# Two tables streamed beside gathers: other tile quotas per step, a gate stage of 22 steps, and second-table loads of four tiles

## The chip, the core and the metric

One core of one Trainium2 chip runs the whole kernel. The metric is the device time of one execution in microseconds (us); the profiled execution is one such execution, with every engine's instructions and every DMA packet recorded. TensorE is PE (its weight loads PEld), VectorE DVE, ScalarE ACT, GpSimd POOL, and SyncE SP, which here does nothing but wait for semaphores and issue DMAs in program order.

## What is computed

One layer of an encoder block: a token mixer (a causal convolution branch and a stick-breaking attention branch, gated and projected) with a layer norm, and then PEER, a retrieval of single-neuron experts, which is what this change is about:

```python
s1, s2 = q1 @ keys_1.T, q2 @ keys_2.T            # 8 heads, 128 keys each
v1, i1 = top_k(s1, 16); v2, i2 = top_k(s2, 16)
top_s, pos = top_k(v1[:, None] + v2[None, :], 16)
idx = (i1 * 128 + i2)[pos]                       # one of 16384 experts
gate = softmax(top_s)
u, vv = expert_u[idx], expert_v[idx]             # rows of 1024 float32
act = gelu(einsum('td,thkd->thk', x, u))
y = einsum('thk,thkd->td', gate * act, vv)
x = layer_norm(ALPHA * x + y)
```

There are 1024 tokens in 8 blocks of 128.

## The kernel before

Six of the eight token blocks get their experts by **gather**. The work of a block and a head is a turn of 8 steps (`TURNS` = 48 turns, `STEPS` = 8, so 384 steps). In each step POOL gathers two experts for each of 128 tokens, rows of 8 KB that hold u and v together (`indirect_dma_start`, L975), into a ring of 8 places, four steps deep; DVE forms the dot products (`dots`, L2430), ACT the weights (`expert_weights`, L1806 to L1815), and PE adds the weighted v rows to the block's sum (`experts`, L1258). A ring place is free when PE has used it.

The last two blocks (`DENSE` = 2) are computed **densely** beside turns 32 to 47, without gathers: all 16384 rows of both tables are streamed through. Steps are counted from there as s, from 0 to 127, and each engine does in each step what `dense` gives it, in program order beside its part of the gathered work.

- **First table** (`u_tile`, L1496): 128 tiles of 128 experts; the products with the 256 tokens go through a gelu (L1957) into `act_out` and, but for the last two chunks, out to DRAM (`store_act`). SP loads two tiles per transfer (`load_u`, L848) into six places. `u_first(s)` says which tiles belong to step s: 128 tiles over `U_STEPS` = 94 steps, evenly. A pair is loaded when tile 2m - 6 + 1 has been used (`u_used`). The third pair waits for `y_read`, since its place holds data of the gathered block 3 until then.
- **Score slabs**: beside turns 30 to 38 PE also forms queries and scores for further heads (L1219, L1243). The two halves of a slab are loaded by SP (`load_slab_late`, L730). The first half may be loaded when the first half of the slab before has been read (`q_psum`), the second when its scores are done (`score_psum`). Slab 13 (`LATE_SLAB + 2`) is the one that PE wants first at step 0. Here SP issues its loads at n = `USLOTS - 1`, behind the third pair.
- **Picks and gates**: from step 0 DVE picks the top experts of the dense blocks (`dense_pick`, four steps per head and block, 64 steps). At `G_STEP0` = 64 PE turns the picks (`turn_picks`). Then the gates are spread to the full table, in 64 groups of four tokens over `G_STEPS` = 24 steps: DVE writes two one-hot matrices (`hot_group`, L2525 and L2529) into one of two places `hot`, PE multiplies them (`g_group`, L1509), ACT copies the result into `g_out` (L1967), and SP stores each block of eight groups, 2 MB, to DRAM (`store_g`, L857). `g_out` has two places; ACT fills one again when its store has landed. SP issues a store at tile `u_first(g_full(i)) + USLOTS` of its own loop, behind the `load_u` of that point.
- **Between the tables**: SP issues the rest of the stores, waits until they have landed, loads the gates of the first two chunks of eight tiles (`load_g`, L879, pieces of 1 KB per partition), and then the first second-table tiles.
- **Second table** (`v_tile`, L332 to L334 by `split_products`): 128 tiles over `V_STEPS` = 31 steps, evenly (`v_first`). Each v tile is rounded by ACT (`round_v`, L1978), the rest is formed by DVE (L2554), and PE makes 12 matmuls of 512 columns. Four tiles at a time the activations are multiplied by their gates (DVE, L2566, two steps ahead of use), rounded by ACT (L1989) and split by DVE (L2548). SP loads two tiles per transfer (`load_v`, L868) into four places of two; a place is loaded again when its two tiles have been used, so pair m waits for 2m - 6 used tiles. Every four tiles come 0.5 MB of activations (`load_act`, L888) and 0.5 MB of gates (`load_g`). In SP's order at one count of used tiles these two come first, and then the pair.
- **Tail**: three steps (`TAIL`) without table tiles, in which DVE finishes the dense blocks and the last gathered one.

ACT and DVE prepare v tiles two ahead of the step (`AHEAD`), and ACT's rounding has four places (`VHI`), so tile n is rounded only after tile n - 4 is used.

## Time and profile before

| | us |
|---|---|
| median of 3 runs | 3004.21 (2998.26 to 3004.87) |
| profiled execution | 3014.1 |
| its span, first to last instruction | 3012.3 |
| PE / DVE / ACT / POOL busy | 2616.7 / 2327.7 / 1223.7 / 971.8 |
| moved by DMA | 1100.76 MB, mean 365 GB/s |

A busy PE is not PE at its peak: ends of matmuls are modelled. "DMA share" is the mean busy share of the 16 DMA engines (it can come out a little over 1), the clock is the one granted to PE, 1.00 being 2.4 GHz and 0.50 being 1.2 GHz. What stands in brackets behind an instruction is the idle time of its engine before it and what ended it.

### The profile page before, as it was taken

Reading aid. Unit: us, or ns where it says so; the run is one execution under the profiler, and the core shown is the slowest. Engines: PE = TensorE matmul, PEld = TensorE weight load, DVE = VectorE, ACT = ScalarE, POOL = GpSimd, SP = SyncE. Lnnn points to the kernel's source line nnn. Section 1 sums busy time; section 2 is a strip of 40 time slices with the busy share of each in tenths; the row PEclk is TensorE's granted clock in tenths of the full one; section 3 lists DMA queues with packets and bytes.
Section 4 is the critical chain, followed back from the end, with each engine's and each line's share of the span. In section 5 each row is a group of like instructions: output and inputs, shape, how many; then the busy total and the mean of one; then the engine's idle time right before and its main releaser. Section 6 shows DMA issues by size and latency. Waiting matters only on the chain. (4 is left out here: it accounts for less than half of the span.)

```text
span 3012.3 us, 53462 instructions
## 1 busy us (share of the span) xinstructions
PE 2616.7 (87%) x20618; PEld 1518.2 (50%) x20618; DVE 2327.7 (77%) x4875; ACT 1223.7 (41%) x3048; POOL 971.8 (32%) x888
## 2 busy tenths in 40 slices
PE   9899978787887767768888869999998997999997
PEld 7677433232332333323333326666676775766774
DVE  7965577999879899976767867767788884877776
ACT  3254143233345555533333423333244332544454
POOL 0000144444445555544343522223232222211221
PEclk9999999889997777779998989999999999999998
DMA  4113699999999999999999989999999999999995
GB/s 165 63 56 140 240 403 419 413 404 417 412 419 405 420 411 420 419 420 421 421 418 406 419 336 383 397 394 401 400 416 375 397 412 411 386 392 369 410 393 210
DMA packets 175382, 1100.76 MB, mean 365 GB/s; under 512 B 17829, under 2 KB 34341, under 8 KB 52778
## 3 DMA queue, kind: packets, MB, share of 16 engines
q0 software_dynamic: 110592, 805.36, 65.3%
q1 hardware_dynamic: 64554, 292.16, 24.5%
q8 instruction: 160, 2.62, 0.3%
q14 instruction: 76, 0.62, 0.1%
HBM read 1061.79 MB, written 35.65 MB: 364 GB/s over the span
## 5 line engine op out<-in xcount | busy, mean ns | idle before, releaser
L975 POOL DMA_INDIRECT arena_high<-uv_dram,idx_now x768 | 929.3, 1210 | 1665.9 <-PE ps L1258 1525.2
L2430 DVE SCALAR_TENSOR_TENSOR arena_high<-arena_low,arena_high 128x1024 f32<-128x1024 f32 x768 | 922.4, 1223 | 267.4 <-DMA arena_high<-uv_dram,idx_now 261.5
L1258 PE MATMUL ps<-arena_high 32*32 32x512 f32 x12288 | 493.5, 671 | 282.5 <-ACT arena_high L1815 278.1
L1496 PE MATMUL ps<-arena_low 128*128 128x256 f32 x2048 | 463.7, 382 | 0.0
L1496 PEld LDWEIGHTS ps<-arena_low 128*128 128x128 f32 x2048 | 384.0, 190 | 109.4 <-issue 46.0
L1806 ACT ACTIVATE gcol<-hcol 128x2 f32<-128x2 f32 x384 | 77.6, 202 | 824.4 <-DVE arena_high L2430 820.0
L1258 PEld LDWEIGHTS ps<-arena_high 32*32 32x32 f32 x12288 | 94.8, 107 | 481.6 <-ACT arena_high L1815 384.6
L1219 PE MATMUL ps<-arena_low 128*128 128x512 f32 (+1 forms) x512 | 242.0, 616 | 14.3 <-DMA arena_low<-slabs_dram 14.3
L332 PE MATMUL ps<-wv_hi_bytes,w_hi_bytes 128*128 128x512 f32 x512 | 207.6, 406 | 19.4 <-DVE v_lo_bytes L2554 13.1
L1815 ACT ACTIVATE arena_high<-arena_high,wcol 128x32 f32<-128x32 f32 x768 | 204.9, 314 | 12.5
L334 PE MATMUL ps<-wv_hi_bytes,w_lo_bytes 128*128 128x512 f32 x512 | 202.3, 395 | 0.0
L1808 ACT ACTIVATE wcol<-gcol,arena_high 128x1 f32<-128x1 f32 x768 | 184.2, 287 | 12.6
L1219 PEld LDWEIGHTS ps<-arena_low 128*128 128x128 f32 x512 | 98.1, 203 | 168.6 <-issue 139.8
L1957 ACT ACTIVATE arena_low<-ps 128x512 f32<-128x512 f32 x64 | 38.2, 596 | 320.9 <-PE ps L1496 320.9
L333 PE MATMUL ps<-x_lo_bytes,w_hi_bytes 128*128 128x512 f32 x384 | 152.0, 396 | 0.0
L332 PEld LDWEIGHTS ps<-wv_hi_bytes,w_hi_bytes 128*128 128x128 f32 x512 | 98.2, 192 | 70.4 <-issue 30.7
L1393 PE MATMUL ps<-arena_low 128*128 128x512 f32 x256 | 126.4, 640 | 0.0
L332 PE MATMUL ps<-x_hi_bytes,w_hi_bytes 128*128 128x512 f32 x256 | 103.9, 406 | 7.2 <-DVE x_lo_bytes L2116 7.1
L334 PEld LDWEIGHTS ps<-wv_hi_bytes,w_lo_bytes 128*128 128x128 f32 x512 | 97.9, 191 | 21.2
L970 POOL CAST idx_now<-arena_high 128x8 uint32<-128x8 f32 x96 | 39.1, 407 | 209.4 <-DVE arena_high L2416 209.0
L2554 DVE TENSOR_TENSOR x_hi_bytes<-arena_low,wv_hi_bytes 128x1024 fp32r<-128x1024 f32 x64 | 76.4, 1223 | 39.0 <-ACT wv_hi_bytes L1978 38.5
L334 PE MATMUL ps<-x_hi_bytes,w_bytes 128*128 128x512 f32 x256 | 101.0, 395 | 0.0
(264 smaller groups left out, 4002.4 us busy)
## 6 DMA issues: line engine op xcount, KB each, us to landing
arena_low<-ut_dram SPq DMA_DIRECT2D x64, 1024.0 KB
arena_high<-vt_dram SPq DMA_DIRECT2D x32, 1024.0 KB, 12.7
arena_low<-vt_dram SPq DMA_DIRECT2D x32, 1024.0 KB
arena_low<-spread_dram SPq DMA_DIRECT2D x32, 512.0 KB
acts_dram<-arena_low SPq DMA_DIRECT2D x14, 1024.0 KB
arena_low<-acts_dram SPq DMA_DIRECT2D x28, 512.0 KB
arena_low<-slabs_dram SPq DMA_DIRECT2D x11, 1152.0 KB
arena_high<-uv_dram,idx_now POOLq DMA_INDIRECT x768
```

The source lines that it names most:

```text
L332: nc.tensor.matmul(out, w_hi, x_hi, start=first, stop=False)
L333: nc.tensor.matmul(out, w_hi, x_lo, start=False, stop=False)
L334: return nc.tensor.matmul(out, w_lo, x_hi, start=False, stop=last)
L975: pool.indirect_dma_start(out=ring[:, s % RING, :], out_offset=None, in_=uv_d, in_offset=bass.IndirectOffsetOnAxis(ap=idx_now[:, s:s + 1], ...
L1219: last = nc.tensor.matmul(ps[:, q_half_bank(i, half), j0 * P:j1 * P], w[:, k, half, :], x1T[:, j0:j1, k, :], start=(k == 0), stop=(k == KD ...
L1258: last = nc.tensor.matmul(ps[out:out + QUAD, y_bank(t // PH) + turn, :], diag[rows, s % DIAGS, :], ring[rows, s % RING, cs], start=fresh, ...
L1393: last = nc.tensor.matmul(ps[:, 4 + g, :], w_mix_late[m % 2][:, o:o + P], xT_late[:, k, :], start=(k == 0), stop=(k == KD - 1))
L1496: last = nc.tensor.matmul(ps[:, 5 + n % 4 // 2, o:o + 2 * P], u_slot[n % USLOTS][:, k, :], x1T[:, BLK - DENSE:BLK, k, :], start=(k == 0), ...
L1806: steps.link(nc.scalar.activation(gcol[:, s0:s0 + 2], hcol[:, s0:s0 + 2], ACT.Gelu))
L1808: last = nc.scalar.activation(wcol[:, s:s + 1], gcol[:, s:s + 1], ACT.Copy, scale=gates[:, t % (BLK * PH), s:s + 1])
L1815: nc.scalar.activation(diag[:, s % DIAGS, :], quad_eye, ACT.Copy, scale=wcol[:, s:s + 1]).then_inc(diag_ready, 1)
L2430: last = nc.vector.scalar_tensor_tensor(out=ring[:, s % RING, 0:D], in0=x1[c][:, j, :], scalar=1.0, in1=ring[:, s % RING, 0:D], op0=ALU.mu ...
```

## The change

Five edits. (1) The two halves of slab 13 are issued at n = `USLOTS - 2`, before the third u pair. (2) `u_first` and `v_first` follow weights: steps 0 to 55 take 133 parts each, the gate steps 113, the other first-table steps 205; second-table steps 0 to 24 take 467 and the last eight 130. First-table steps are 92, second-table steps 33. (3) Gate groups take 22 steps instead of 24, PE's and ACT's from step 65 and DVE's from step 64, with four `hot` places. (4) The first four gate loads are issued at tile `u_first(G_BACK) + USLOTS - 2` in SP's loop over the first table, `G_BACK` being 88. (5) The second table is loaded four tiles per transfer, with 16 KB in a row in DRAM, into two places of 16 KB per partition. Load m waits for 4m - 4 used tiles, and in SP's order comes before the activation and gate loads of the same count.

```diff
-V_STEPS = 31
+V_STEPS = 33
+V_FULL = 25
...
-G_STEP0 = PICK0 + DENSE * PH * PICK_PARTS - U0
-G_STEPS = 24
+G_STEP0 = PICK0 + DENSE * PH * PICK_PARTS - U0 + 1
+G_STEPS = 22
+HOTS = 4
 KEPT = 2
+G_BACK = G_STEP0 + G_STEPS + 1
...
+def u_share(s):
+
+    G = U0 + s
+    if G < PICK0 + 7 * STEPS:
+        return 133
+    return 113 if G_STEP0 <= s < G_STEP0 + G_STEPS else 205
...
 def u_first(s):
-    return NT * s // U_STEPS
+    return NT * sum(u_share(i) for i in range(s)) // sum(u_share(i) for i in range(U_STEPS))
+
+
+def v_share(v):
+    return 467 if v < V_FULL else 130
...
 def v_first(v):
-    return NT * v // V_STEPS
+    return NT * sum(v_share(i) for i in range(v)) // sum(v_share(i) for i in range(V_STEPS))
...
-        v_pair = [at(kib, 2, D) for kib in (168, 176, 64, 72)]
+        v_quad = [at(kib, 4, D) for kib in (168, 64)]
...
-        hot = at(16, 2, 4, 2 * P)
+        hot = [at(kib, 4, 2 * P) for kib in (16, 20, 28, 32)]
...
-                if m == VSLOTS // 2 - 1:
+                if m == 1:
                     wait_again(sp_eng, u_used, NT)
-                if m >= VSLOTS // 2:
-                    wait_again(sp_eng, v_used, 2 * m - VSLOTS + 2)
-                sp_eng.dma_start(v_pair[m % (VSLOTS // 2)], vt_d[v_expert(2 * m) // 2, :, :, :]).then_inc(v_in[m % (VSLOTS // 2)].sem, 16)
+                if m >= 2:
+                    wait_again(sp_eng, v_used, 4 * m - VSLOTS + 4)
+                sp_eng.dma_start(v_quad[m % 2], vt_d[v_expert(4 * m) // 4, :, :, :]).then_inc(v_in[m % 2].sem, 16)
...
             for n in range(NT):
+                if n == USLOTS - 2:
+                    for half in range(2):
+                        load_slab_late(LATE_SLAB + 2, half)
                 if n % 2 == 0:
                     load_u(n // 2)
...
+                if n == u_first(G_BACK) + USLOTS - 2:
+                    for c in range(2):
+                        for part in range(2):
+                            load_g(c, part)
...
-            for c in range(2):
-                for part in range(2):
-                    load_g(c, part)
...
-                if n % 2 == 0:
-                    load_v(n // 2)
+                if n % 4 == 0:
+                    load_v(n // 4)
...
-                if s == G_STEP0:
+                if s == G_STEP0 - 1:
                     for j in range(DENSE):
                         turn_picks(j)
...
-                wait_again(act, v_in[n // 2 % (VSLOTS // 2)], 16 * (n // VSLOTS + 1))
+                wait_again(act, v_in[n // 4 % 2], 16 * (n // VSLOTS + 1))
...
-                if i >= 2:
-                    wait_again(dve, g_psum, i - 1)
+                if i >= HOTS:
+                    wait_again(dve, g_psum, i - HOTS + 1)
...
-                o = s - G_STEP0
+                o = s - G_STEP0 + 1
```

## Rows read from the trace of the kernel before

**Rows 1.** Windows by stage: length, busy us (instructions) per engine, granted clock, DMA share, GB/s.

```profile
1773.00:1787.00 14.00, 0.00 (x0) 0.00 (x0) 13.21 (x45) 1.22 (x5) 0.00 (x0) 0.60 0.98 406
1787.00:1794.00 7.00, 6.93 (x11) 3.16 (x12) 6.65 (x20) 0.00 (x0) 0.00 (x0) 0.58 0.06 23
1794.00:2228.00 434.00, 434.00 (x3331) 291.94 (x3329) 307.77 (x895) 156.57 (x427) 119.15 (x123) 1.00 0.97 390
2228.00:2295.00 67.00, 61.08 (x543) 42.04 (x528) 51.71 (x144) 23.76 (x67) 21.22 (x21) 0.95 1.01 422
2295.00:2508.00 213.00, 198.40 (x1728) 158.31 (x1727) 183.60 (x503) 86.99 (x239) 50.87 (x51) 1.00 0.97 391
2508.00:2566.00 58.00, 39.91 (x352) 28.52 (x338) 22.91 (x52) 15.99 (x42) 13.48 (x15) 0.87 1.01 412
2566.00:2937.00 371.00, 353.69 (x2222) 264.06 (x2223) 288.55 (x377) 185.36 (x295) 78.23 (x63) 0.97 0.99 390
2937.00:2983.00 46.00, 44.88 (x291) 33.85 (x305) 30.46 (x35) 21.27 (x37) 7.67 (x6) 1.00 0.78 308
2983.00:3012.00 29.00, 10.21 (x152) 1.79 (x120) 20.30 (x30) 9.96 (x19) 0.00 (x0) 0.64 0.14 55
```

**Rows 2.** Groups of instructions, 2295 to 2508: count | busy, mean ns | idle before, releaser.

```profile
L2529 DVE TENSOR_SCALAR arena_low<-iota,arena_low 128x128 f32<-128x128 f32 x248 | 69.6, 347 | 0.0
...
L2525 DVE TENSOR_TENSOR arena_low<-iota,arena_low 128x512 f32<-128x512 f32 x62 | 42.7, 688 | 27.6 <-PE ps L1509 27.2
...
L1509 PE MATMUL ps<-arena_low 128*128 128x128 f32 x496 | 65.8, 281 | 14.6 <-DVE arena_low L2529 14.5
```

**Rows 3.** The page of the whole execution: its first line.

```profile
span 3012.3 us, 53462 instructions
```

**Rows 4.** Timeline of PE, 1744 to 1800 and the last u tiles: start, us, line, count.

```profile
1748.06 2.84 PE L1219 MATMUL ps<-arena_low 128*128 128x512 f32 x6
...
1762.56 2.05 PE L1243 MATMUL ps<-arena_low 128*128 128x128 f32 x16
...
1787.07 6.57 PE L1219 MATMUL ps<-arena_low 128*128 128x512 f32 x8 [14.34 <-DMA arena_low<-slabs_dram]
...
1798.09 3.70 PE L1219 MATMUL ps<-arena_low 128*128 128x512 f32 x8
...
2538.54 7.17 PE L1496 MATMUL ps<-arena_low 128*128 128x256 f32 x32
```

**Rows 5.** Chain of waits in the second table: two expert groups, a step apart.

```profile
2603.94 1.07 PE ps L1258 x32
...
2616.12 1.07 PE ps L1258 x32
```

**Rows 6.** Timeline of SP around step 0: start, us until the last issue, line, DMA, count.

```profile
1715.85 58.53 SPq L848 DMA_DIRECT2D arena_low<-ut_dram  x3
1774.42 0.91 SPq L730 DMA_DIRECT2D arena_low<-slabs_dram  x2
```

**Rows 7.** Chain of waits between the tables, in order of time: start, us, what.

```profile
2512.63 18.24 DMA spread_dram<-arena_low
...
2532.46 10.56 SPq L879
2543.07 20.28 DMA arena_high<-vt_dram
```

**Rows 8.** The copies into `g_out` (L1967), all of them: what ACT waited for.

```profile
  PE ps L1509: 71.0, 63
```

**Rows 9.** Timeline of DVE in the same stretch.

```profile
2558.00 1.23 DVE L2566 TENSOR_TENSOR arena_low<-arena_low 128x1024 f32<-128x1024 f32 x1 [21.86 <-DMA arena_low<-spread_dram]
```

**Rows 10.** Rounding and subtraction of v tiles: count: duration ns min/median/max, first, last start.

```profile
L1978 ACT ACTIVATE wv_hi_bytes<-arena_low x64: 1038/1045/1065, 2573.4 to 2972.0; 128x1024 fp32r<-128x1024 f32 x64
...
L2554 DVE TENSOR_TENSOR x_hi_bytes<-arena_low,wv_hi_bytes x64: 1217/1224/1228, 2574.8 to 2973.1; 128x1024 fp32r<-128x1024 f32 x64
```

**Rows 11.** DMAs from `vt_dram`, two tiles each: time from issue to landing, us.

```profile
DMA to landing us min/median/max: 8.0/12.7/16.7
```

More of the change, by code:

```diff
@@ L603, in build @@
         g_stored = [Again(wv_in, 16), Again(bv_in, 16)]
-        v_in = [Again(wbranch_in[i], 32) for i in range(VSLOTS // 2)]
+        v_in = [Again(wbranch_in[i], 32) for i in range(2)]
         v_rounded = Again(gates_done, 16)
@@ L891, in _ @@
             for n in range(NT):
+                if n == USLOTS - 2:
+                    for half in range(2):
+                        load_slab_late(LATE_SLAB + 2, half)
                 if n % 2 == 0:
                     load_u(n // 2)
-                for i in range(LATE_SLAB + 2, len(SLABS)):
-                    s0 = (i - LATE_SLAB - 3) * STEPS
-                    if n == (USLOTS - 1 if s0 < 0 else u_first(s0 + 2) + USLOTS):
+                for i in range(LATE_SLAB + 3, len(SLABS)):
+                    s0 = (i - LATE_SLAB - 3 + 32) * STEPS - U0
+                    if n == u_first(s0 + 2) + USLOTS:
                         load_slab_late(i, 0)
-                    if n == (USLOTS - 1 if s0 < 0 else u_first(s0 + 7) + USLOTS):
+                    if n == u_first(s0 + 7) + USLOTS:
                         load_slab_late(i, 1)
@@ L1508, in g_group @@
                 for q in range(4):
-                    last = nc.tensor.matmul(ps[:, (4, 7)[i % 2], q * P:(q + 1) * P], hot[:, i % 2, q, 0:P],
-                                            hot[:, i % 2, q, P:2 * P], start=True, stop=True, skip_group_check=True)
+                    last = nc.tensor.matmul(ps[:, (4, 7)[i % 2], q * P:(q + 1) * P], hot[i % HOTS][:, q, 0:P],
+                                            hot[i % HOTS][:, q, P:2 * P], start=True, stop=True, skip_group_check=True)
                 last.then_inc(g_psum.sem, 1)
@@ L1997, in dense @@
                 s = G - U0
-                if s == G_STEP0:
+                if s == G_STEP0 - 1:
                     for j in range(DENSE):
@@ L2520, in hot_group @@
                     wait_again(dve, picks_ready, DENSE)
-                if i >= 2:
-                    wait_again(dve, g_psum, i - 1)
+                if i >= HOTS:
+                    wait_again(dve, g_psum, i - HOTS + 1)
                 j = i // (P // 4)
                 t0 = 4 * i - j * P
-                nc.vector.tensor_tensor(hot[:, i % 2, :, 0:P], iota128[:, :].unsqueeze(1).to_broadcast([P, 4, P]),
+                nc.vector.tensor_tensor(hot[i % HOTS][:, :, 0:P], iota128[:, :].unsqueeze(1).to_broadcast([P, 4, P]),
                                         picksT[:, j, 1, t0:t0 + 4].unsqueeze(2).to_broadcast([P, 4, P]), ALU.is_equal)
@@ L2528, in hot_group @@
                     t = t0 + q
-                    last = nc.vector.tensor_scalar(hot[:, i % 2, q, P:2 * P], iota128[:, :], picksT[:, j, 0, t:t + 1],
+                    last = nc.vector.tensor_scalar(hot[i % HOTS][:, q, P:2 * P], iota128[:, :], picksT[:, j, 0, t:t + 1],
                                                    picksT[:, j, 2, t:t + 1], ALU.is_equal, ALU.mult)
@@ L2787 @@
         "ut": arr(peer_u).reshape(NKEY // 2, 2, NKEY, KD, P).transpose(0, 4, 1, 3, 2).reshape(NKEY // 2, P, 2, D),
-        "vt": arr(peer_v).reshape(NKEY // 2, 2, NKEY, D).transpose(0, 2, 1, 3),
+        "vt": arr(peer_v).reshape(NKEY // 4, 4, NKEY, D).transpose(0, 2, 1, 3),
         "cols": np.concatenate([col(bi[0:col_v]), col(bi[col_g:]), col(arr(conv_b_pw2)), col(arr(conv_b_dw)),
```

## The prediction

> **What bounds the kernel now.** I read the windows by stage first [rows 1]: they show, per stage, how long PE was busy, its granted clock and how full the 16 DMA engines were. From 1794 on both are full at once: PE 434.00 of 434 with DMA share 0.97, then 61 of 67 with 1.01, 198 of 213 with 0.97, 354 of 371 with 0.99. So neither alone "is" the bound; a change can only win back time in which both stood still or one stood for a reason of its own. There are four such places: 1773 to 1794, where PE did nothing for 14.3 us and DMA then stood still (23 GB/s); the gate stage 2295 to 2508 with 14.6 us of PE idle before its gate matmuls [rows 2]; the joint 2508 to 2566 between the two tables (PE 40 of 58 us); and the end of the second table, 2937 to 2983, where DMA falls to 0.78. After 2983 a serial tail of 29 us remains that the change does not touch. The profiled execution took 3014.1 us around a span of 3012.3 [rows 3]; the median of the timed runs is 3004.2. I sum against the span and carry the difference over to the median.
>
> **Prices.** Two first-table tiles (u tiles) in a row take 7.17 us of PE, 3.6 each [rows 4]. One step and four second-table tiles (v tiles) take 12.18 us, from one expert group at 2603.94 to the next at 2616.12, of which the expert group is 1.07: 2.78 us for a v tile [rows 5]. A gate group is 65.8/62 = 1.06 us on PE and (69.6+42.7)/62 = 1.81 us on DVE [rows 2]. A gather step and a u tile move 2.1 and 0.52 MB; at the 390 to 420 GB/s of [rows 1] that is 5.1 and 1.3 us of DMA. All bytes stay as they are.
>
> **1. Slab 13 ahead of the third u pair.** SP sits in L848 from 1715.85 until the pair is issued about 1774.0, since that pair waits for `y_read`; the two halves of slab 13 come behind it at 1774.42 [rows 6], and PE, in order, waits 14.34 us for them and then runs its first eight passes at the low clock, 6.57 us instead of 3.70 [rows 4]. Moved ahead, the halves wait for slab 12's use alone: its first half is read for the last time about 1749 to 1751, its scores end at 1764.6 [rows 4]. Both halves are on their way 10 to 25 us earlier, and PE needs the first at 1773 and the second some three steps later. Queued behind the moved waits is only the third pair, which has to wait until 1774 anyway. Gain 14.3 + 2.9 = 17.2 us on PE; nothing else is late there, since DMA stood still too. Bounds: 10 (the second half late by a few us) to 17.
>
> **2. Tiles by step.** The quota sums give 74 u tiles after step 55 (76 before), 92 after step 64 (88 at this point before), 117 after the last gate step, 128 after step 91 (before 93). Steps 0 to 55 are paced by PE [rows 1]: 1773 to 2228 is 455 us, minus 17.2, minus two tiles 7.1: 431. DMA needs for this stretch some 56 x 5.1 + 70 x 1.3 + slabs and stores near 45 = 422, so it just keeps up. Steps 56 to 64: 67 us before with 12 tiles and two gate groups; now 18 tiles and none: +6 x 3.6 - 2.1 = 86.5, less part of the 6 us that PE idled: 83 (78 to 88).
>
> **3. Gates in 22 steps with four `hot` places.** Before, DVE stands 27.6 us in front of L2525 for PE, and PE 14.6 us for DVE [rows 2]: with two places each waits for the other in turn. With four places, and DVE one step ahead, this falls away. What is late next: DVE needs 183.6 - one step's 3.3 + two groups 3.6 = 184 us, PE 25 tiles x 3.65 + 64 x 1.06 + 22 x 1.1 = 183, DMA 22 gather steps, 25 tiles, 16.8 MB of gate stores: 79 MB at 410 = 193. Floor 188 to 193 against 213 (for 23 steps and 31 tiles). But ACT may fill a `g_out` place again only when its store has landed, and a store takes 18.24 us [rows 7]. SP issues it after a `load_u` that waits for PE: by the new quotas blocks 0, 4 and 5 leave only with the first tile of the step after the one in which they do now, while a block of eight groups takes 2.75 steps instead of 3. Today no fill waits for DMA: the only releaser of L1967 is PE [rows 8]. For these blocks I get 5 to 10 us each of ACT standing, with PE behind it at the next group, partly absorbed because DVE and DMA run on: +10 (0 to 25). Stage: 203.
>
> **4. Gate loads before the last u tiles.** Before, u tiles ended at 2545.7 [rows 4], and the first v tile waited for a chain: store 18.24, SP's wait in L879, v pair 20.28 [rows 7]; DVE stood 21.86 us at L2566 for the gate load, with the next dots behind it in order [rows 9]. Now tiles 117 to 127 and five expert groups are 11 x 3.6 + 5.4 = 45 us. The wait for the stores moves into SP's queue at tile 123. Behind it stand the last two `load_u`, and behind these v quad 0. PE has tiles to about 24 us past tile 117; store (18) and 2 MB of gate pieces in 1 KB runs (10 to 18, they share the engines with gathers) and one u pair (3) make 31 to 39. PE stands 8 to 16 us, instead of the 18 before; but quad 0 lands while the last four u tiles run. Joint: 57 (48 to 68), against 58 with two fewer tiles and one step more before.
>
> **5. Second table.** Steps 0 to 24 take 4.70 tiles, the last eight 1.31. PE work is 128 x 2.78 + 33 x 1.07 = 391 us (before 389, measured 417 from 2566 to 2983). DMA's work moves from the last steps to where PE works: a long step asks for 5.1 + 4.7 x 1.95 = 14.3 us of DMA and 14.1 of PE, a short one 7.6 and 4.7 (a v tile with its act and gate pieces is 0.79 MB, 1.95 us), while the gathers end four steps before the end. What DMA lost in 2937 to 2983, 0.22 x 46 = 10 us, can mostly be used. Against it, a place of four tiles is only asked for again when all four are used, so the next tile but three has 4 x 2.78 + 1.07 = 12.2 us from issue to use, where a pair had six tiles, 17.7 us. To this belong rounding and subtraction, 1.05 + 1.22 [rows 10]. **The landing of 2 MB is in no row.** Lower bound: the quickest pair, 8.0 us for 1 MB; upper: the slowest, 16.7, plus 1 MB more at 410 GB/s, 2.6: 19.3 [rows 11]. I take 10.5, near the low end, for the slow pairs stand behind an act and a gate load issued in the same burst, and the quad comes ahead of them: 2 MB at full rate 5.1 plus at most one step's gathers beside it 5.1, and a little to start. Use is then possible at 12.8: 0.6 us late, and as two places alternate, half of it counts: 29 x 0.3 = 8.7 us. What is behind it: ACT's rounding in order blocks its next expert weights, DVE's L2554 its next dots. Act and gate pieces now land after the quad; the multiply L2566 sometimes has three tiles (9 us) of lead instead of four. -10 + 2 + 8.7 = +0.7: 417 stays (400 to 450). Taking 32 issues away from SP is worth nothing: SP mostly waits.
>
> The Trainium skill ("DMA: Bandwidth & Descriptors", section "Anatomy of one DMA — SWDGE (gpsimd) path") puts one transfer at about 2.0 us plus bytes over 436 GB/s. By that estimate a quad lands in 6.8 us and is never late, and the 8.7 us of my sum would be 0, which is the v stage of rival (c) below. The row speaks against using it here: a lone pair would be 4.4 by the same fit, and the quickest measured is 8.0, the median 12.7 [rows 11].
>
> **Sum.** 1773 + 431 + 83 + 203 + 57 + 417 + 29.5 = 2993.5 against 3012.3: -18.8. Median: 3004.2 - 18.8 = 2985.4, say 2985.5.
>
> **Rivals.** (a) *Quads come late, slower.* If a quad lands in 14.5 us, use is at 16.8, the period of four tiles is (12.2 + 16.8)/2 = 14.5 instead of 12.2: +2.3 x 29 = 67, instead of my 9, of which some 15 are hidden as DMA is the slower anyway: +43 on the sum, 3028. It decides from a landing of about 12.7 us, where (15.0 - 12.2)/2 x 29 = 41 less 15 eats my 19. For it: median pair 12.7, multiply already waits for gate pieces in the saturated stretch; against: place in the burst, and that gathers per tile fall by 12%. 0.12. (b) *Only the start is gained:* stores hold up the gates by 20, the joint gives nothing, v stage +5: -17 + 15 = about 3002. 0.13. (c) *Every cover holds:* gates at 190, joint 50, v stage at DMA's floor 405: 2985.5 - 13 - 7 - 12 = 2954. 0.13. (d) *The slab move does nothing*, because half 1 lands late and PE stands as long: +14, 2999.5. 0.03. My forecast, as summed, 0.59.
>
> **Chances and range.** Likeliest 2985.5; its own bounds (start 10 to 17, gates 0 to 25, joint 48 to 68, v 400 to 450) give about 2966 to 3003. With 2 in 10 left out, below from (c) and above from (a): 2962 to 3010. A measurement can tell about 0.2%, 6 us. Faster than 2998.2: forecast, (c) and a little of (b): 0.76. Within 0.2%: 0.13. Slower than 3010.2: 0.11.
>
> **What would show it.** Right: no PE wait for a slab near 1773, and DMA never at rest there; L2525 no longer released by PE; first v tile near 2547; no step of the last eight over 8 us. Wrong: `arena_low<-spread` stores releasing L1967 for more than 25 us in all; PE idle before L332 over 50 us with `vt_dram` behind ACT's rounding; quads landing above 13 us. If steps 0 to 55 don't get shorter by 17 us besides the two tiles, DMA and not PE paced them.

## The result, and the profile after

The kernel after takes 3035.24 us (median of 5 runs, 3030.86 to 3041.04), the kernel before in the same comparison 3004.87 us (2998.26 to 3011.85): ratio 1.0094, 95% interval [1.0082, 1.0106]. The change makes the kernel slower by 0.9%, some 28 us; the prediction said 2985.5 us. The profiled execution took 3041.0 us.

Lines have moved: L848, L868, L879 and L1219 of before are L863, L883, L894 and L1238 after, L1258, L1496, L1509 are L1277, L1515, L1528, L1967, L1978 and L1989 are L1986, L1997 and L2008, the weights L1806 to L1815 are L1825 to L1834, L2430, L2525, L2554, L2566 are L2449, L2544, L2573, L2585, and PE's L332 to L334 are L347 to L349.

The page of the kernel after, against [rows 3] and [rows 11]: its first line, the group of the u tiles (its idle time at the end), and the DMA issues (size of one, median us from issue to landing).

```profile
span 3038.9 us, 53432 instructions
...
L1515 PE MATMUL ps<-arena_low 128*128 128x256 f32 x2048 | 465.8, 384 | 16.6 <-DMA arena_low<-ut_dram 16.6
...
arena_high<-vt_dram SPq DMA_DIRECT2D x16, 2048.0 KB, 9.8
arena_low<-vt_dram SPq DMA_DIRECT2D x16, 2048.0 KB, 10.5
arena_low<-spread_dram SPq DMA_DIRECT2D x32, 512.0 KB, 13.8
```

The four-tile loads (quads) land in about 10 us, which is what the prediction had assumed. The windows by stage, in the columns of [rows 1]:

```profile
1773.00:1794.00 21.00, 21.00 (x148) 12.71 (x160) 19.24 (x62) 3.40 (x12) 3.75 (x4) 0.98 1.01 408
1794.00:2205.00 411.00, 411.00 (x3181) 275.65 (x3149) 309.11 (x897) 154.11 (x420) 121.14 (x119) 1.00 0.99 400
2205.00:2283.00 78.00, 76.66 (x609) 57.38 (x608) 51.34 (x143) 26.18 (x69) 21.15 (x21) 1.00 1.01 416
2283.00:2476.00 193.00, 178.82 (x1617) 143.74 (x1616) 181.43 (x502) 82.16 (x236) 59.30 (x49) 0.97 0.97 400
2476.00:2541.00 65.00, 46.48 (x342) 35.48 (x337) 17.22 (x34) 12.08 (x33) 10.90 (x12) 0.87 0.88 349
2541.00:2944.00 403.00, 359.37 (x2113) 267.07 (x2114) 282.28 (x373) 181.94 (x278) 65.92 (x54) 0.95 0.88 341
2944.00:3010.00 66.00, 56.65 (x464) 38.29 (x479) 42.51 (x57) 28.23 (x66) 25.71 (x20) 0.97 0.99 388
3010.00:3038.00 28.00, 9.52 (x152) 1.79 (x120) 20.09 (x30) 10.50 (x20) 0.00 (x0) 0.67 0.18 71
```

Up to the first v tile the kernel after is ahead: 2541.0 against 2565.8. The bubble at 1773 is gone (PE 21 of 21 us, DMA 1.01). Then the second table takes 468.6 us (2541.0 to 3009.6) instead of 417.0, and in it neither engine nor DMA is full: PE 359 of 403, DMA share 0.88 and 341 GB/s where [rows 1] had 0.99 and 390. So waits pace it, and not the throughput of PE or DMA.

The waits of that stretch (2541 to 2955; engine, what, releaser: total us, times, longest) point at the loads. ACT, before its rounding, stood 48.6 + 46.1 us for v loads in 24 waits, 10.0 us at the longest. The kernel before has such waits too, 66.0 us in 31 between 2566 and 2983, but none over 7.5 us. The rows after:

```profile
ACT w_hi_bytes L2008 <- DVE arena_low L2585: 75.8, 24, 8.5
DVE x_hi_bytes L2573 <- ACT wv_hi_bytes L1997: 54.7, 17, 8.7
ACT wv_hi_bytes L1997 <- DMA arena_high<-vt_dram: 48.6, 12, 9.2
DVE x_lo_bytes L2573 <- ACT wv_hi_bytes L1997: 48.1, 13, 8.8
ACT wv_hi_bytes L1997 <- DMA arena_low<-vt_dram: 46.1, 12, 10.0
```

One such wait, step by step. Quad 12 (tiles 48 to 51) is issued at 2696.50, when tile 43 has been used, and lands at 2706.8. The timeline of ACT (start, us, what, count, and in brackets the idle time before it):

```profile
2706.81 1.06 ACT L1997 ACTIVATE wv_hi_bytes<-arena_high 128x1024 fp32r<-128x1024 f32 x1 [9.19 <-DMA arena_high<-vt_dram]
2710.30 1.06 ACT L2008 ACTIVATE w_hi_bytes<-arena_low 128x1024 fp32r<-128x1024 f32 x1 [2.43 <-DVE arena_low L2585]
2712.59 0.20 ACT L1825 ACTIVATE gcol<-hcol 128x2 f32<-128x2 f32 x1 [1.23 <-DVE arena_high L2449]
2712.83 0.48 ACT L1827 ACTIVATE wcol<-gcol,arena_high 128x1 f32<-128x1 f32 x2
2713.34 0.53 ACT L1834 ACTIVATE arena_high<-arena_high,wcol 128x32 f32<-128x32 f32 x2
2713.78 2.94 ACT L1997 ACTIVATE wv_hi_bytes<-arena_high 128x1024 fp32r<-128x1024 f32 x3
```

of DVE:

```profile
2707.91 1.23 DVE L2573 TENSOR_TENSOR x_lo_bytes<-arena_high,wv_hi_bytes 128x1024 fp32r<-128x1024 f32 x1 [8.83 <-ACT wv_hi_bytes L1997]
2709.05 1.22 DVE L2585 TENSOR_TENSOR arena_low<-arena_low 128x1024 f32<-128x1024 f32 x1
2710.18 1.22 DVE L2449 SCALAR_TENSOR_TENSOR arena_high<-arena_low,arena_high 128x1024 f32<-128x1024 f32 x1
```

and of PE:

```profile
2709.28 0.47 PE L347 MATMUL ps<-wv_hi_bytes,w_hi_bytes 128*128 128x512 f32 x1 [0.64 <-DVE x_lo_bytes L2573]
...
2716.13 0.79 PE L347 MATMUL ps<-wv_hi_bytes,w_hi_bytes 128*128 128x512 f32 x1 [3.85 <-DVE x_lo_bytes L2573]
2716.72 0.63 PE L348 MATMUL ps<-x_lo_bytes,w_hi_bytes 128*128 128x512 f32 x1
```

Tile 48, the quad's first, is the last that ACT and DVE prepare in their step. PE gets it only 0.64 us late. But ACT and DVE stood some 9 us for it, and behind it, in program order, come the multiply (2709.05), the rounding of its result (2710.30), the next step's two dots (from 2710.18) and weights (2712.59), and only then the rounding of tiles 49 to 51 (2713.78), 7.0 us after they landed. So the tile that is late is 49, by 3.85 us. Over the whole stage PE's idle time before the first matmul of tiles 4m, 4m + 1, 4m + 2 and 4m + 3 adds up to 10.1, 18.9, 14.4 and 4.6 us: most of it before tiles that are not the first of their quad. The Trainium skill ("PSUM — Partial Sum Buffer", section "Engine vs sequencer instructions") calls the queues of ScalarE and VectorE strictly first in, first out. These rows agree: tile 49 was there at 2706.8 and was rounded at 2713.78, behind all that stood before it.

### The profile page after: what moved, and what is told of

Same layout as the page of the kernel before. It is cut to its first block and busy times, and to the rows that moved or that the text cites. A ratio compares the mean times of both kernels' runs of the same rounds, so it can differ in the third digit from the quotient of the medians.

```text
span 3038.9 us, 53432 instructions
## 1 busy us (share of the span) xinstructions
PE 2636.7 (87%) x20618; PEld 1532.6 (50%) x20618; DVE 2325.2 (77%) x4875; ACT 1220.3 (40%) x3050; POOL 990.7 (33%) x888
## 5 line engine op out<-in xcount | busy, mean ns | idle before, releaser
L994 POOL DMA_INDIRECT arena_high<-uv_dram,idx_now x768 | 949.5, 1236 | 1681.8 <-PE ps L1277 1540.4
L2449 DVE SCALAR_TENSOR_TENSOR arena_high<-arena_low,arena_high 128x1024 f32<-128x1024 f32 x768 | 922.2, 1223 | 279.8 <-DMA arena_high<-uv_dram,idx_now 273.8
L1277 PE MATMUL ps<-arena_high 32*32 32x512 f32 x12288 | 492.7, 670 | 256.0 <-ACT arena_high L1834 253.2
L1515 PE MATMUL ps<-arena_low 128*128 128x256 f32 x2048 | 465.8, 384 | 16.6 <-DMA arena_low<-ut_dram 16.6
L1515 PEld LDWEIGHTS ps<-arena_low 128*128 128x128 f32 x2048 | 386.1, 191 | 125.8 <-issue 62.8
L1825 ACT ACTIVATE gcol<-hcol 128x2 f32<-128x2 f32 x384 | 77.6, 202 | 870.2 <-DVE arena_high L2449 869.8
L1277 PEld LDWEIGHTS ps<-arena_high 32*32 32x32 f32 x12288 | 94.2, 107 | 457.4 <-ACT arena_high L1834 367.6
L347 PE MATMUL ps<-wv_hi_bytes,w_hi_bytes 128*128 128x512 f32 x512 | 213.7, 417 | 47.9 <-DVE x_hi_bytes L2573 16.6
L1238 PE MATMUL ps<-arena_low 128*128 128x512 f32 (+1 forms) x512 | 241.4, 615 | 0.0
L1834 ACT ACTIVATE arena_high<-arena_high,wcol 128x32 f32<-128x32 f32 x768 | 204.8, 314 | 12.5
L349 PE MATMUL ps<-wv_hi_bytes,w_lo_bytes 128*128 128x512 f32 x512 | 206.3, 403 | 0.0
L1238 PEld LDWEIGHTS ps<-arena_low 128*128 128x128 f32 x512 | 98.1, 204 | 155.7 <-issue 144.7
L347 PEld LDWEIGHTS ps<-wv_hi_bytes,w_hi_bytes 128*128 128x128 f32 x512 | 100.6, 197 | 105.0 <-issue 40.4
L2573 DVE TENSOR_TENSOR x_hi_bytes<-arena_low,wv_hi_bytes 128x1024 fp32r<-128x1024 f32 x64 | 75.5, 1222 | 62.6 <-ACT wv_hi_bytes L1997 62.4
L349 PEld LDWEIGHTS ps<-wv_hi_bytes,w_lo_bytes 128*128 128x128 f32 x512 | 100.6, 196 | 22.6
L347 PE MATMUL ps<-x_hi_bytes,w_hi_bytes 128*128 128x512 f32 x256 | 103.8, 406 | 7.3 <-DVE x_lo_bytes L2135 7.3
L348 PE MATMUL ps<-x_hi_bytes,w_hi_bytes 128*128 128x512 f32 x256 | 102.0, 398 | 0.0
## 6 DMA issues: line engine op xcount, KB each, us to landing
arena_low<-vt_dram SPq DMA_DIRECT2D x16, 2048.0 KB, 10.5
arena_high<-uv_dram,idx_now POOLq DMA_INDIRECT x768, 12.2
```

Of the source, the lines that this page charges most:

```text
L347: nc.tensor.matmul(out, w_hi, x_hi, start=first, stop=False)
L348: nc.tensor.matmul(out, w_hi, x_lo, start=False, stop=False)
L349: return nc.tensor.matmul(out, w_lo, x_hi, start=False, stop=last)
L994: pool.indirect_dma_start(out=ring[:, s % RING, :], out_offset=None, in_=uv_d, in_offset=bass.IndirectOffsetOnAxis(ap=idx_now[:, s:s + 1], ...
L1238: last = nc.tensor.matmul(ps[:, q_half_bank(i, half), j0 * P:j1 * P], w[:, k, half, :], x1T[:, j0:j1, k, :], start=(k == 0), stop=(k == KD ...
L1277: last = nc.tensor.matmul(ps[out:out + QUAD, y_bank(t // PH) + turn, :], diag[rows, s % DIAGS, :], ring[rows, s % RING, cs], start=fresh, ...
```

## The experiments

Each edit is against the kernel named. "Quads" are loads of four tiles, "pairs" those of two, the period is the time of four tiles, taken from tile 16 to tile 112 (24 periods). Ratios are to the kernel before.

**Theory and rivals.** Theory: the quads cost the second table its 52 us. Rivals: the tile quotas do (4.70 tiles a step), or something ahead of the v tiles.

### Quads or quotas

`e1_pairs`: the kernel after with pairs again.

```diff
-        v_quad = [at(kib, 4, D) for kib in (168, 64)]
+        v_pair = [at(kib, 2, D) for kib in (168, 176, 64, 72)]
...
-                    wait_again(sp_eng, v_used, 4 * m - VSLOTS + 4)
+                    wait_again(sp_eng, v_used, 2 * m - VSLOTS + 2)
...
-                if n % 4 == 0:
-                    load_v(n // 4)
+                if n % 2 == 0:
+                    load_v(n // 2)
```

> The kernel after, with second-table loads of two tiles as before (four places, pair m waits for 2m - 6 used tiles, activations and gates ahead of the pair that is issued at the same count); the other four edits stay. Theory Q (the loads of four tiles cost the v stage its 53 us, 470 instead of the 417 forecast): the v stage falls back to 415 to 430 and the kernel to about 2985 to 2995 us. Rival T (the tile quotas cost it: 4.70 tiles per long step with rounding only two tiles ahead): it stays at 3020 to 3035. Rival G (what costs is in the joint or the gate stage, before the v tiles): 3025 to 3035 as well, but with the v stage at 420.

Measured 2996.42 us, ratio 0.9964 [0.9948, 0.9979]: faster than before, and 39 us less than after. Second table 424.8 us, period 12.79 us against 14.38. From 2541 to 2903:

```profile
2541.00:2903.00 362.00, 346.22 (x2114) 261.91 (x2115) 282.93 (x373) 183.98 (x282) 66.60 (x54) 0.97 0.97 379
```

`e2_quads_alone`: the kernel before with edit 5 alone.

```diff
-        v_pair = [at(kib, 2, D) for kib in (168, 176, 64, 72)]
+        v_quad = [at(kib, 4, D) for kib in (168, 64)]
...
-                    wait_again(sp_eng, v_used, 2 * m - VSLOTS + 2)
+                    wait_again(sp_eng, v_used, 4 * m - VSLOTS + 4)
```

> The kernel before with edit 5 alone (loads of four tiles into two places). Theory Q: 3004 plus 35 to 55 us, 3040 to 3060, with PE standing before v tiles some 40 us longer than before. Rival T (quotas cost): 3000 to 3010, no change that can be told.

Measured 3058.69 us, ratio 1.0163 [1.0141, 1.0186]: second table 457.2 us instead of 417.0, period 14.04 against 13.18. Both directions agree: edit 5 is the cause. It changes three things at once, the size of a load, the moment of the request and its place in SP's order, taken apart under "Size, request, order".

`e3_even_v`: the kernel after with even v quotas.

```diff
 def v_share(v):
-    return 467 if v < V_FULL else 130
+    return 1
```

> The kernel after, with the 128 v tiles spread evenly over its 33 second-table steps (3.88 a step) instead of 4.70 in 25 steps and 1.31 in eight. Rival T: the v stage comes back to 420 to 430 and the kernel to 2990 to 3000. Theory Q: the loads stay late, gains less than 10 us here or loses the DMA time of the last steps again: 3025 to 3045.

Measured 3029.39 us, ratio 1.0061 [1.0043, 1.0080]. The rival that blamed the quotas for the whole loss falls; they cost some 6 to 10 us of it (second table 459.1 us against 468.6). `e7_pairs_even_v` has the same edit on the kernel with pairs.

> The kernel after with pair loads and with v tiles spread evenly over the 33 steps. It prices the v quotas without the four-tile loads. The prediction's step gave 10 us of DMA time to the quotas: then this is 8 to 12 us slower than the pairs experiment, about 3006. Rival: in the pairs experiment the last 16 tiles and 12 steps took 63 us against 49 for 16 tiles and 4 steps before, so the short last steps give it back: within 5 us of the pairs experiment, 2992 to 3000.

Measured 2988.95 us, ratio 0.9947 [0.9933, 0.9962], against 0.9964 [0.9948, 0.9979] with the quotas. That is below both ranges: the 10 us that the prediction gave to the quotas have the wrong sign, and the rival was the nearer one. The short last steps win nothing. They fill DMA (0.98 against 0.81 from tile 112 on), but the last 16 tiles take 63 us instead of 48.

### Size, request, order

`e4_two_at_once`: pairs, both issued at the quad's moment.

```diff
-                    wait_again(sp_eng, v_used, 2 * m - VSLOTS + 2)
+                    wait_again(sp_eng, v_used, 4 * (m // 2) - VSLOTS + 4)
...
-                if n % 2 == 0:
-                    load_v(n // 2)
+                if n % 4 == 0:
+                    load_v(n // 2)
+                    load_v(n // 2 + 1)
```

> As the experiment with pairs, but both pairs of a group of four tiles are issued together, at the moments of the four-tile load (both wait for 4k - 4 used tiles, ahead of the activations and gates of that count). It tells the late request from the large transfer. If what costs is that all four tiles land as one transfer, the first pair lands 2.5 us or more earlier and the kernel is near the one with pairs, 2985 to 3000. If what costs is the late request and its place ahead of activations and gates, it is near the kernel after, 3025 to 3040.

Measured 3026.52 us, ratio 1.0052 [1.0033, 1.0070], period 13.95 us. The first pair lands in 7.4 us (median of the 27 loads whose landing the trace tells), some 3 us before a quad; this gives back 9 of the 39 us.

`e11_pairs_lead_four`: `e1_pairs` with each pair asked for two tiles later.

```diff
-                    wait_again(sp_eng, v_used, 2 * m - VSLOTS + 2)
+                    wait_again(sp_eng, v_used, 2 * m - VSLOTS + 4)
```

> The kernel after with pair loads, but every pair waits for 2m - 4 used tiles instead of 2m - 6, so that it has the lead of the four-tile load (four tiles, 12.2 us) with half its bytes. Theory of the lead: as slow as the four-tile loads or slower, 3025 to 3050, with ACT's rounding standing for vt_dram at nearly every pair. Rival S (the size of one transfer): near the pairs experiment, 2996 to 3005.

Measured 3038.12 us, ratio 1.0097 [1.0074, 1.0120], period 14.35 us: the whole loss without any quad, although these pairs land in 8.9 us (median of the 16 that the profile tells, of 64). So a shorter lead from request to use is enough for the loss, and the size of a transfer isn't needed for it.

`e5_quads_behind`: meant to issue the quads behind the activations and gates of their count.

```diff
-            for n in range(NT):
+            for n in range(-2, NT):
...
-                if n % 4 == 0:
-                    load_v(n // 4)
+                if n % 4 == 2 and (n + 2) // 4 < NT // 4:
+                    load_v((n + 2) // 4)
```

> The kernel after, four-tile loads kept, but in SP's order each stands behind the activation and gate loads of the same count of used tiles instead of ahead of them. The two-pairs experiment gave back 9 of the 39 us that pairs give back, so about 30 us belong to the late request and its place. Theory L (the v tiles themselves are late: request at four used tiles instead of two or three before): the quad now starts some 2 us later and gets slower or stays, 3033 to 3055 us. Rival W (activation and gate pieces landing 12 to 16 us after issue, behind the quad, hold the multiply and with it DVE's dots): 3010 to 3025.

Measured 3033.32 us, ratio 1.0094 [1.0079, 1.0110], the same as after. It had to be: the edit doesn't do what its expectation says. At n = 4m - 2 it puts quad m behind the loads of that n, and there it stood already, since SP has nothing to issue between that n and 4m; the two traces show SP's 319 DMAs in the same order. So this run repeats the kernel after, and the order wasn't tested. Against the gate pieces, which the prediction suspected, speak other rows: DVE stood for them (`arena_low<-spread_dram`) 14.2 us in 4 waits in the whole stage, and `e9_quads_aligned` below, with the same order in SP, loses nothing.

### Where the load falls in a step

The lead explains why the quad is awaited, but not the price: by the prediction's sum a quad 0.6 us late costs 9 us. The rows above suggest the place of the wait in the step. `e9_quads_aligned` keeps the quads and gives every step the four tiles of one quad to prepare.

```diff
 def v_first(v):
-    return NT * sum(v_share(i) for i in range(v)) // sum(v_share(i) for i in range(V_STEPS))
+    return 0 if v <= 0 else min(4 * v - 2, NT)
```

> The kernel after, four-tile loads kept, but v_first is 0, 2, 6, 10 and so on: with preparation two tiles ahead, each step's ACT and DVE work is then just the four tiles of one load. Theory B (what costs is not the landing time but where it falls: ACT waits for the load in the middle of a step's list, and the next step's dots, weights and the load's other tiles stand in line behind it): the v stage falls from 469 to 410 to 435, the kernel to 2980 to 3005. Rival L (lateness of the load by itself, whatever the step's list): no change beyond the 6 us that the even quotas gave, 3025 to 3035.

Measured 2987.99 us, ratio 0.9931 [0.9910, 0.9953]: 47 us less than after, and faster than the kernel before, with the same quads landing in the same time (median 10.4 us, of the 19 whose landing the trace tells). Even steps alone (`e3_even_v`) gave 6 of the 47 us. ACT's timeline of one step:

```profile
2683.26 3.90 ACT L1997 ACTIVATE wv_hi_bytes<-arena_low 128x1024 fp32r<-128x1024 f32 x4 [1.41 <-DMA arena_low<-vt_dram]
2690.15 1.06 ACT L2008 ACTIVATE w_hi_bytes<-arena_low 128x1024 fp32r<-128x1024 f32 x1 [2.99 <-DVE arena_low L2585]
2692.50 0.20 ACT L1825 ACTIVATE gcol<-hcol 128x2 f32<-128x2 f32 x1 [1.28 <-DVE arena_high L2449]
...
2695.87 3.90 ACT L1997 ACTIVATE wv_hi_bytes<-arena_high 128x1024 fp32r<-128x1024 f32 x4 [2.09 <-DMA arena_high<-vt_dram]
```

and the stage, over the same 403 us as that of after:

```profile
2541.00:2944.00 403.00, 386.10 (x2482) 282.63 (x2481) 314.43 (x419) 206.46 (x333) 68.10 (x71) 1.00 1.00 397
```

All four tiles are rounded in one go as soon as they are there. ACT still stands for loads, 55.2 us in 25 waits, but never over 4.0 us, and the load's other three tiles stand right behind the first. PE stands about 0.2 us for a quad (median; 17.6 us for all 32), DMA is at 1.00. `e13_quads_off_by_one` shifts the steps by one tile, with equal steps of four kept, so that each step prepares three tiles of a quad and the first of the next.

```diff
-    return NT * sum(v_share(i) for i in range(v)) // sum(v_share(i) for i in range(V_STEPS))
+    return 0 if v <= 0 else min(4 * v - 1, NT)
```

> As the aligned four-tile kernel, but v_first is 0, 3, 7, 11 and so on: still four tiles a step, but the last tile that a step prepares is the first of the next load. Theory B (place of the load in the list): the worst case, since after each landing a step's multiply, dots and weights come before the load's second tile, some 7 us in each period: v stage 460 to 490, kernel 3030 to 3055. Rival E (equal steps of four were what helped): 2985 to 2995, as with 0, 2, 6, 10.

Measured 3106.56 us, ratio 1.0331 [1.0316, 1.0347], beyond what was expected: second table 535.4 us, period 16.95 against 12.90. One tile of shift costs 119 us in this kernel. The window of the stage:

```profile
2541.00:2944.00 403.00, 328.85 (x1924) 239.11 (x1923) 250.41 (x346) 159.10 (x256) 56.28 (x56) 0.91 0.80 313
```

and ACT's timeline of one step in it:

```profile
2700.70 1.06 ACT L1997 ACTIVATE wv_hi_bytes<-arena_high 128x1024 fp32r<-128x1024 f32 x1 [10.09 <-DMA arena_high<-vt_dram]
2704.19 1.06 ACT L2008 ACTIVATE w_hi_bytes<-arena_low 128x1024 fp32r<-128x1024 f32 x1 [2.43 <-DVE arena_low L2585]
...
2707.67 2.93 ACT L1997 ACTIVATE wv_hi_bytes<-arena_high 128x1024 fp32r<-128x1024 f32 x3
```

Here ACT rounds a quad's second tile 7 us after its first in each step, as with quad 12 of the kernel after; with 4.70 tiles a step it does so in some. The price falls on every second quad, where ACT stands 10 to 11 us, and PE about 2 us before the first tile and about 4 before the second. Not all of the 119 us is order: the quads land later here, 12.6 us against 10.4 (median), for a reason that wasn't found. Quad 14 shows what that is worth: it is issued at 2755.06, and quad 16, which waits for the last tile of quad 14, 33.47 us later, so that 2 us of landing lengthen two periods by 2 us. That makes an estimated 30 of the 119 us. `e10_pairs_aligned` has the aligned steps with pairs.

> The same quotas (0, 2, 6, 10 and so on) with pair loads. Theory B: with pairs the load is early enough in most steps, so little is left to win: v stage 408 to 417, kernel 2980 to 2990, against 2989 with even quotas. Rival: DMA at a share of 1.00 holds the v stage at 417 whatever the order: 2987 to 2991.

Measured 2982.25 us, ratio 0.9910 [0.9894, 0.9926]; against `e9_quads_aligned` the price of quads as such is at most some 6 us, and the two intervals overlap. PE's idle time before the first tile of four is 16.3 us here and 17.6 with quads.

### The other edits

`e6_slab_alone`: the kernel before with edit 1 alone.

```diff
+                if n == USLOTS - 2:
+                    for half in range(2):
+                        load_slab_late(LATE_SLAB + 2, half)
                 if n % 2 == 0:
                     load_u(n // 2)
-                for i in range(LATE_SLAB + 2, len(SLABS)):
+                for i in range(LATE_SLAB + 3, len(SLABS)):
```

> The kernel before with edit 1 alone: slab 13 issued ahead of the third u pair. The step of the prediction (17.2 us of PE, nothing else late there) expects 17 us less than before, ratio 0.9943, all of it kept to the end. Rival: steps 0 to 55 are then paced by DMA and part comes back as DMA backlog: 5 to 12 us less.

Measured 2990.38 us, ratio 0.9947 [0.9935, 0.9960]: 15 to 16 us less, kept to the end. This one edit alone does as well as `e7_pairs_even_v` with all of edits 1, 3, 4 and the first-table quotas.

`e8_pairs_two_hots`: `e1_pairs` with two places.

```diff
-HOTS = 4
+HOTS = 2
```

> The kernel after with pair loads and two hot places instead of four; 22 gate steps and DVE one step ahead stay. The prediction's step (with two places DVE and PE wait in turn, 14.6 us of PE) expects 8 to 15 us more than the pairs experiment, 3005 to 3011. Rival: DVE being a step ahead is enough, and the places are worth nothing: within 3 us.

Measured 3130.54 us, ratio 1.0419 [1.0404, 1.0434]. Both expectations fall. The gate stage takes 330 us instead of 193; rows from 2280 to 2610:

```profile
L1528 PE MATMUL ps<-arena_low 128*128 128x128 f32 x512 | 83.8, 326 | 109.0 <-ACT arena_low L1986 55.6 <-ACT arena_high L1986 53.4
...
L2544 DVE TENSOR_TENSOR arena_low<-iota,arena_low 128x512 f32<-128x512 f32 x62 | 42.8, 690 | 142.3 <-PE ps L1528 142.0
...
L1825 ACT ACTIVATE gcol<-hcol 128x2 f32<-128x2 f32 x23 | 4.7, 203 | 204.7 <-DVE arena_high L2449 204.7
```

and the window:

```profile
2281.00:2608.00 327.00, 218.01 (x1598) 165.16 (x1612) 182.87 (x499) 78.63 (x230) 42.31 (x49) 0.80 0.65 243
```

With two places and DVE one step ahead, three engines wait in a ring. DVE stands for PE to multiply a group of the step before (142 us); the dots of its own step stand behind that. ACT stands for these dots (205 us), with its copies of the gate products behind them, and PE stands for the copies (109 us) before it multiplies the next group. So the four places are what makes "a step ahead" possible, not a gain beside it.

`e12_pairs_even_late_gates`: `e7_pairs_even_v` with edit 4 undone, the gate loads behind all first-table loads again.

```diff
-                if n == u_first(G_BACK) + USLOTS - 2:
-                    for c in range(2):
-                        for part in range(2):
-                            load_g(c, part)
...
                 if u_first(g_full(i)) + USLOTS >= NT:
                     store_g(i)
+            for c in range(2):
+                for part in range(2):
+                    load_g(c, part)
```

> The kernel with pair loads and even v quotas, with edit 4 undone: the first four gate loads are issued after all first-table loads again. In the joint of the kernel after DMA moved 349 GB/s against 414 before. Theory J (the early gate loads, waiting for the stores in SP's queue, hold the v loads and gathers back): the joint is at 400 GB/s or more and the kernel 3 to 8 us faster, 2981 to 2986. Rival: the multiply L2585 waits for the gate load again and the first v tile moves from 2541 to 2550 to 2560: 5 to 15 us slower, 2994 to 3004.

Measured 2980.80 us, ratio 0.9910 [0.9894, 0.9927] against 0.9947 [0.9933, 0.9962]: the early gate loads cost 8 to 11 us. SP's timeline in the joint of the kernel after (start, us until the last issue, line) shows how:

```profile
2480.10 0.91 SPq L872 DMA_DIRECT2D spread_dram<-arena_low  x2
2499.44 11.05 SPq L894 DMA_DIRECT2D arena_low<-spread_dram  x4
2510.54 1.67 SPq L863 DMA_DIRECT2D arena_low<-ut_dram  x2
2512.25 0.43 SPq L883 DMA_DIRECT2D arena_high<-vt_dram  x1
```

SP waits in L894 for the stores, and the last two first-table pairs stand behind it until 2510.5. PE waits 16.6 us for `ut_dram`, and DMA is at 0.88. With the loads behind, the last u tile ends at 2517.3 instead of 2538.0 and the first v tile starts at 2529.7 instead of 2541.0 (2537.8 and 2540.7 in `e7_pairs_even_v`). DVE stands longer for the gate loads then, 28.4 us against 19.2 in that kernel, and it costs less than PE's wait for u tiles.

Three combinations: `e14_pairs_aligned_late_gates` (pairs, aligned steps, late gate loads), `e15_quads_aligned_late_gates` (the same with quads) and `e16_before_slab_aligned` (`e6_slab_alone` with aligned steps, old gates). The first two join the diffs above; the third adds to that of `e6_slab_alone`:

```diff
-V_STEPS = 31
+V_STEPS = 33
...
-    return NT * v // V_STEPS
+    return 0 if v <= 0 else min(4 * v - 2, NT)
```

> Pair loads, aligned steps and late gate loads together. If the gains of aligned steps (7 us against even ones) and of late gate loads (8 us) add: 2973 to 2976 us. If both only fill the same DMA time: 2978 to 2983.

> As the run before it, with four-tile loads. The four-tile loads cost 6 us beside aligned steps with early gate loads; the same here gives 2979 to 2985. If they cost more in the joint, where the second load waits for the last first-table tile: 2985 to 2992.

> The kernel before with the slab move and 33 second-table steps of 0, 2, 6, 10 and so on tiles; first-table tiles evenly over 92 steps, gates over 24 steps with two hot places, pair loads. If edits 2 and 3 in the first table are worth what the stages show (5 us at the first v tile, against two more steps behind it): 2980 to 2986. If they are worth the 10 us that the prediction gave to the gate stage: 2985 to 2992.

Measured 2975.94 us, ratio 0.9897 [0.9883, 0.9912]; 2982.45 us, 0.9915 [0.9902, 0.9928]; and 2987.70 us, 0.9928 [0.9915, 0.9941]: the first two in the lower of their ranges, the third in the upper. The first beats both kernels of this case, by 30 and 59 us. Against the third it shows that edit 3 and the first-table quotas together are worth some 9 to 12 us once the gate loads are late; the slab move gives more than that alone.

## Why the prediction was wrong

The sum by its own terms, from the profiled execution (us; a stage ends with PE's expert group):

| | predicted | measured |
|---|---|---|
| 1773 to step 55 | 431 | 432.0 |
| steps 56 to 64 | 83 | 77.8 |
| gate stage | 203 | 193.2 |
| joint | 57 | 65.0 |
| second table | 417 | 468.6 |
| tail | 29.5 | 29.3 |

**Step 1, slab 13: right in size.** 17.2 us expected; 15 to 16 in the run with this edit alone. Its reason ("DMA stood still too") holds only for the 7 us behind PE's stop, with DMA at 0.06; beside the stop itself DMA was at 0.98 [rows 1]. The room for the gain was there and in the 434 us that follow, where DMA goes from 0.97 to 1.00 in `e6_slab_alone` at the same length. PE's timeline, beside [rows 4], has the first passes at full clock and without a wait:

```profile
1773.50 3.79 PE L1238 MATMUL ps<-arena_low 128*128 128x512 f32 x8
1777.13 3.62 PE L1515 MATMUL ps<-arena_low 128*128 128x256 f32 x16
```

**Step 3, gates: mechanism right, its price wrong.** ACT does wait for stores now, as forecast, where [rows 8] had only PE, and DVE's wait for PE falls from 27.6 us [rows 2] to 9.4. The groups of the gate stage, 2268 to 2476:

```profile
L1528 PE MATMUL ps<-arena_low 128*128 128x128 f32 x512 | 66.6, 283 | 14.2 <-ACT arena_low L1986 8.9 <-ACT arena_high L1986 5.3
L2544 DVE TENSOR_TENSOR arena_low<-iota,arena_low 128x512 f32<-128x512 f32 x64 | 43.9, 686 | 9.4 <-PE ps L1528 9.0
L1986 ACT ACTIVATE arena_low<-ps 128x256 f32<-128x256 f32 x64 | 20.4, 381 | 21.4 <-DMA spread_dram<-arena_low 12.7 <-PE ps L1528 8.6
L1986 ACT ACTIVATE arena_high<-ps 128x512 f32<-128x512 f32 x32 | 18.5, 593 | 22.0 <-DMA spread_dram<-arena_high 12.0 <-PE ps L1528 10.0
```

ACT stood 24.7 us for stores, at the top of the range given, and yet the stage took the 193 us that the prediction had as DMA's floor: the added 10 us were not seen. DMA at 0.97 paced it, as far as the rows tell: 193 us at 400 GB/s are 77 MB, near the 79 MB of the prediction's floor (the terms that it lists add up to 76). PE's idle before its gate matmuls stayed at 14 us, with another releaser.

**Step 4, joint: right that PE would stand for the last u pairs (16.6 us, 8 to 16 expected), 8 us too short in all, and wrong in not seeing the loads' late place as the better one** (the joint takes 56.7 us in `e12_pairs_even_late_gates`). The row that it rests on, DVE's 21.86 us before L2566 [rows 9], was idle time in a stretch in which DMA was at 1.01 [rows 1], so little was to be had there; with the early loads DMA is at 0.88 instead.

**Step 5, second table: this is where the prediction failed.** It said 417 us (400 to 450), and 468.6 were measured. Its landing time was right (10.5 assumed, 10.2 measured as the median), and so, in a kernel where nothing stands between a load's first tile and its others, was its small price of a quad 0.6 us late: aligned, 0.2 us of PE for a quad, and 416.1 us for the stage. The step that failed is the one sentence on what is behind the wait ("ACT's rounding in order blocks its next expert weights, DVE's L2554 its next dots"), which named the right thing and put no number on it. The trace after gives one: multiply, rounding of its result, two dots and the weights, 7.0 us between the landing of a quad and the rounding of its second tile. With this, the quad's second tile needs 10.3 + 7.0 + 2.3 = 19.6 us from the request, as measured (2696.50 to 2716.13), and has 12.2 + 2.8 = 15.0. The sum held 8.7 us for late quads in place of the 40 to 44 that they cost (`e2_quads_alone`, `e1_pairs`). The gain of 10 us from DMA in the last steps was not there either (`e7_pairs_even_v`).

**Rival (a)** had the right sign and mechanism, late quads, and was given 0.12, since it counted the first tile of a quad alone and so decided only from a landing of 12.7 us. The measured landing is below that, and the result, 3035, above its 3028. By the Trainium skill's fit ("DMA: Bandwidth & Descriptors", section "Anatomy of one DMA — SWDGE (gpsimd) path") a quad would land in an estimated 6.8 us; the quickest here took 7.5 us and the median was 10.2, so the trace doesn't agree, and ACT stood for quads 24 times in this stage. That section is on transfers which GpSimd issues, and these are SyncE's, beside gathers that keep DMA near full; no run here shows a lone transfer.

**What stays open.** The 44 us between quads and pairs with the same quotas (468.6 and 424.8) are 53.0 us of idle PE against 24.3, and 15 us more of busy PE for the same matmuls, at a granted clock of 0.95 against 0.98. The second table whole, after and with pairs:

```profile
2541.00:3009.60 468.60, 415.62 (x2568) 305.18 (x2572) 324.45 (x429) 209.77 (x344) 91.63 (x74) 0.95 0.90 348
2541.10:2965.80 424.70, 400.40 (x2568) 298.71 (x2572) 325.19 (x429) 209.63 (x339) 93.52 (x74) 0.98 0.97 381
```

How the 29 us of idle time split into the work behind a landing and the landings of 12 us that some quads had wasn't separated, nor what the place of a quad in SP's order is worth. The gain of aligned steps with pairs (0.9910 against 0.9947) was measured and not explained row by row; the intervals just stay apart.

## What to carry to other kernels

When a load is made larger or later, don't price the lateness of its first tile alone: go through the program order of each engine that waits for it, add up what stands behind the wait until the load's next tile is served, and compare that with the lead. Where a load's tiles are used over steps, let a load's boundary be a step's boundary: here one tile of shift cost 119 us, more than all the edits of the change gave or took. Before an engine's idle time is counted as a gain, look at DMA's share beside it and behind it: in the joint, at 1.01, ending DVE's wait gave nothing, while the slab move gave 15 to 16 us, since DMA had room in what follows. Last, compare the order of issues in the trace before a run is read as a test of it: one of these edits left it as it was.

## What the runs showed of the hardware

A stop of PE can cost more than its length. After the 3.85 us without work that end at 2716.13, six of the seven matmuls of L347 to L349 in the next 3.1 us take 0.63 us or more, and then 0.40 again. The granted clock of these 3.1 us is 0.50, the lower of its two levels (1.2 GHz), and 1.00 (2.4 GHz) from 2719.3 on:

```profile
2716.13:2719.20 3.07, 3.07 (x7) 2.48 (x8) 2.22 (x2) 0.58 (x1) 0.00 (x0) 0.50 0.93 390
```

Behind the stop of 0.64 us at 2709.28 it stayed at 1.00. The granted clock of the same 403 us, a mean of the two levels, goes with the stops: 1.00 in `e9_quads_aligned`, 0.95 after, 0.91 in `e13_quads_off_by_one`. And in this mix of loads and gathers the size of a load didn't set its landing time: pairs of 1 MB landed in 12.7 us [rows 11], 10.4 (`e1_pairs`) and 8.9 (`e11_pairs_lead_four`), quads of 2 MB in 10.2 after, 10.4 in `e9_quads_aligned` and 12.6 in `e13_quads_off_by_one` (medians). That what is queued beside a load sets it is likely, and no run shows it.
